# A 31-tap depthwise convolution split into even and odd phases: three half-length chains on VectorE

## What is computed

```
xn = RMSNorm(x)
[q|k|v|o|i|f|u|g] = xn @ w_in
branch A: mLSTM, 4 heads x 256, chunks of tokens in turn (w = exp(logd - m_tok), C_new = decay*C + ...)
branch B: glu = u[..., :1024] * sigmoid(u[..., 1024:])
          c, conv_buf = causal_dwconv(glu, conv_buf, conv_dw, conv_b)     # width 31, per channel
          c = silu(layernorm(c)); yb = c @ w_proj_b + b_proj_b
merge, output projection, residual, then an FFN: up-projection, depthwise conv of width 3, gelu gate, down
```

## Time and profile before

| | |
|---|---|
| time, median of 3 runs | 1942.17 us (1935.84, 1942.17, 1943.59) |
| span of the profiled execution | 1933.8 us, 31692 instructions |
| TensorE | busy 1914.8 us, 99% |
| VectorE | busy 1308.3 us, 68%; 331.7 us of it in L2241 |
| ScalarE | busy 817.0 us, 42% |
| the chain that ended last | TensorE 90%, VectorE 6%, ScalarE 2% |

### The profile page before, as it was taken

How to read it: one execution, slowest core, us unless ns; L and a number is a source line. 1 busy time by engine, 2 the same in 40 slices (tenths; PEclk the granted TensorE clock), 3 DMA queues, 4 the chain that set the end, 5 groups by cost and what they waited for, 6 DMA issues and landing times.

```text
span 1933.8 us, 31692 instructions
## 1 busy us (share of the span) xinstructions
PE 1914.8 (99%) x12999; PEld 1891.8 (98%) x12999; DVE 1308.3 (68%) x1767; ACT 817.0 (42%) x1512; POOL 81.2 (4%) x138
## 2 busy tenths in 40 slices
PE   9999999999999999999999999999999999999997
PEld 8999999999999999999999999999999999999997
DVE  7788779878788745355444458977777777646363
ACT  5454443233232234474122345655445444645342
POOL 0000001111111111110000000000000000000000
PEclk9999999999999999999999999999999999999999
DMA  3323234343333446659231314222122222556554
GB/s 134 129 97 128 75 126 105 89 100 86 96 92 93 109 118 195 197 171 325 104 136 44 128 39 139 73 84 79 68 89 76 71 79 98 202 189 215 203 175 154
DMA packets 100463, 237.57 MB, mean 123 GB/s; under 512 B 16348, under 2 KB 51548, under 8 KB 100320
## 3 DMA queue, kind: packets, MB, share of 16 engines
q1 hardware_dynamic: 89088, 194.65, 29.6%
q0 software_dynamic: 11232, 40.90, 9.3%
HBM read 182.92 MB, written 52.59 MB: 122 GB/s over the span
## 4 chain that ended last, share of the span: by engine, by line
PE 90%; DVE 6%; ACT 2%; issue 1%; DMA 1%; SPq 0%; POOL 0%; DVEq 0%; ACTq 0%; POOLq 0%
PE ps L1013 14%; PE ps L1015 14%; PE ps L1014 14%; PE ps L1370 7%; PE ps L1371 7%; PE ps L1372 7%; PE ps L1388 4%; PE ps L1390 4%; PE ps L1389 4%; PE ps L1170 3%; PE ps L1171 3%; PE ps L1172 3%; PE ps L1102 1%; PE ps L1099 1%; PE ps L1082 1%
## 5 line engine op out<-in xcount | busy, mean ns | idle before, releaser
L1013 PE MATMUL ps<-rx,fhi 128*128 128x364 f32 (+2 forms) x1312 | 438.8, 334 | 1.0 <-DMA flo<-wts 0.6
L1015 PE MATMUL ps<-rx,flo 128*128 128x364 f32 (+2 forms) x1312 | 427.5, 326 | 0.0
L1014 PE MATMUL ps<-rx,fhi 128*128 128x364 f32 (+2 forms) x1312 | 427.5, 326 | 0.0
L2241 DVE SCALAR_TENSOR_TENSOR cacc<-glub,pars,cacc 128x1118 f32<-128x1118 f32 x240 | 331.7, 1382 | 6.7
L1013 PEld LDWEIGHTS ps<-rx,fhi 128*128 128x128 f32 x1312 | 246.8, 188 | 3.3 <-ACT spl L1560 1.6
L1014 PEld LDWEIGHTS ps<-rx,fhi 128*128 128x128 f32 x1312 | 246.9, 188 | 1.5
L1015 PEld LDWEIGHTS ps<-rx,flo 128*128 128x128 f32 x1312 | 246.6, 188 | 0.0
L1388 PE MATMUL ps<-ghi,dhi 128*128 128x384 f32 (+1 forms) x528 | 173.6, 329 | 1.9 <-DVE glo L2669 1.6
L1390 PE MATMUL ps<-ghi,dlo 128*128 128x384 f32 (+1 forms) x528 | 172.6, 327 | 0.0
L1389 PE MATMUL ps<-glo,dhi 128*128 128x384 f32 (+1 forms) x528 | 172.6, 327 | 0.0
L2662 DVE TENSOR_TENSOR dlo<-draw,dhi 128x1408 fp32r<-128x1408 f32 x48 | 77.7, 1624 | 118.2 <-ACT dhi L1944 118.2
(11 more groups left out here) (339 smaller groups left out, 4839.8 us busy)
## 6 DMA issues: line engine op xcount, KB each, us to landing
draw<-wdn SPq DMA_DIRECT2D x48, 704.0 KB, 4.2
uraw<-wts SPq DMA_DIRECT2D x44, 512.0 KB, 4.3
fhi<-wts POOLq DMA_DIRECT2D x39, 512.0 KB, 6.4
flo<-wts POOLq DMA_DIRECT2D x39, 512.0 KB, 5.6
fraw<-wts SPq DMA_DIRECT2D x27, 512.0 KB, 3.6
scr_g<-cva SPq DMA_DIRECT2D x22, 512.0 KB, 2.6
araw<-wts SPq DMA_DIRECT2D x36, 256.0 KB, 2.7
graw<-scr_g SPq DMA_DIRECT2D x43, 192.0 KB, 4.1
```

Of the source, the lines that this page charges most:

```text
L1013: pe.matmul(b, hi[:, w], src[:, his[k], cols], start=(k == 0), stop=False)
L1014: pe.matmul(b, hi[:, w], src[:, los[k], cols], start=False, stop=False)
L1015: mm = pe.matmul(b, lo[:, w], src[:, his[k], cols], start=False, stop=(k == KB - 1))
L2241: op = dve.scalar_tensor_tensor(a[:, :], g[:, j:j + AW], pars[:, at:at + 1], a[:, :], ALU.mult, ALU.add)
```

## The change

The convolution is computed in two phases. With E = g at even positions and O = g at odd positions (574 each, `GH`), and w0 the 16 even-numbered and w1 the 15 odd-numbered taps, three sums of half length (559, `AH`) are kept:

- f_a = sum of w0[i] * E[m + i] (16 taps)
- f_d = sum of w1[i] * O[m + i] (15 taps, 560 long)
- f_e = sum of (w0[i] + w1[i - 1]) * (E + O)[m + i] (16 taps), on the sum f_s = E + O formed once per block

Even results are f_a[m] + f_d[m] + b; odd results are f_e[m] + b - f_d[m + 1] - f_a[m]. The tap sums `hsum` are formed once at the start. A block is now `NOP` = 51 operations of half length where it was 31 of full length. E and O are read by stride 2 (8 bytes) out of `glub`, and the last two operations write `cacc` by stride 2; f_a, f_d, f_e and f_s are contiguous. The three chains take turns, and each operation waits for the one three back, its own chain's last.

Further: there is one `cacc` in place of two, and the last two operations of block k wait for the store of block k - 1; the row `nb` is now two buffers of [128, 128], loaded for each step two steps ahead by a DMA of 64 KB (36 of them in place of 4, each behind a wait for VectorE's `w_neg`); `TAPS_AT` puts 6 operations ahead of the pair stage, 6 into pair 0, 11 into each other pair and 2 behind it; blocks 2 to 7 put 3 or 4 operations into each slot; `conv_fin` counts two per block.

```diff
@@ constants
+CE = (CW + 1) // 2
+CO = CW // 2
+NOP = 1 + CE + CO + CE + 3
+GH = GW // 2
+AH = AW // 2
-TAPS_AT = [4] + [7 + 6 * i for i in range(NB)]
+TAPS_AT = [6] + [12 + 11 * i for i in range(NB)]
...
-            return [(k, i * CW // CONV_SLOTS, (i + 1) * CW // CONV_SLOTS)]
+            return [(k, i * NOP // CONV_SLOTS, (i + 1) * NOP // CONV_SLOTS)]
...
@@ SyncE
             def store_conv(j):
-                sp.wait_ge(conv_fin, j + 1)
+                sp.wait_ge(conv_fin, 2 * j + 2)
...
+            def load_nb(i):
+                h, j = STEPS[i]
+                sp.dma_start(nb[i % 2][:, :], scr_neg[h][step_cols(j)].partition_broadcast(P)).then_inc(nb_in[i % 2], 16)
...
                     h, j = STEPS[i]
-                    if j == NCHUNK and h + 1 < NH:
+                    if i + 2 < len(STEPS):
                         sp.wait_ge(w_neg, i + 1)
-                        sp.dma_start(nb[:, :], scr_neg[h + 1].partition_broadcast(P)).then_inc(nb_in, 16)
+                        load_nb(i + 2)
...
@@ VectorE
             rest(0)
             x_norm(0), x_rest(0)
+            dwt = pars[:, PDW:PFF].rearrange("p (k j) -> p k j", j=CW)
+            dve.tensor_copy(hsum[:, :, 0:1], dwt[:, :, 0:1]).then_inc(half_set, 1)
+            dve.tensor_tensor(hsum[:, :, 1:CE], dwt[:, :, 1:CW - 1:2], dwt[:, :, 2:CW:2], ALU.add).then_inc(half_set, 1)
             rest(1), rest(2)
...
+            def conv_op(k, n):
+                g = glub[k % 2]
+                g0, g1 = g[:, 0:GW:2], g[:, 1:GW:2]
+                even, odd = cacc[:, 0:AW:2], cacc[:, 1:AW:2]
+                done = (NOP - 2) * k
+                at, q = PDW + k * CW, PV["convb"] + k
+                bias = pars[:, q:q + 1]
+                if n == 0:
...
+                    dve.tensor_tensor(f_s[:, :], g0, g1, ALU.add).then_inc(tap, 1)
+                elif n < NOP - 3:
+                    i, chain = divmod(n - 1, 3)
+                    if i == CE - 1 and chain == 1:
+                        chain = 2
+                    acc, src, w, tapw = (
+                        (f_a, g0, AH, pars[:, at + 2 * i:at + 2 * i + 1]),
+                        (f_d, g1, AH + 1, pars[:, at + 2 * i + 1:at + 2 * i + 2]),
+                        (f_e, f_s, AH, hsum[:, k, i:i + 1]))[chain]
+                    if i:
+                        dve.wait_ge(tap, done + (n - 2 if (i, chain) != (CE - 1, 2) else n - 1))
+                        dve.scalar_tensor_tensor(acc[:, :], src[:, i:i + w], tapw, acc[:, :], ALU.mult, ALU.add).then_inc(tap, 1)
...
+                elif n == NOP - 2:
+                    if k:
+                        dve.wait_ge(c_sto[(k - 1) % 2], 32 * ((k + 1) // 2))
+                        dve.wait_ge(csum_set, k)
+                    dve.scalar_tensor_tensor(even, f_a[:, :], bias, f_d[:, 0:AH], ALU.add, ALU.add).then_inc(conv_fin, 1)
+                else:
+                    dve.wait_ge(tap, done + NOP - 2)
+                    dve.tensor_tensor(odd, f_e[:, :], f_a[:, :], ALU.subtract).then_inc(conv_fin, 1)
```

More of the change, by code:

```diff
@@ L188, in taps_of @@
     while t0 < t1:
-        k, j = divmod(t0, CW)
-        n = min(CW - j, t1 - t0)
+        k, j = divmod(t0, NOP)
+        n = min(NOP - j, t1 - t0)
         yield k, j, j + n
@@ L196, in taps_at @@
     if S_B <= s < S_B + 4:
-        at, rest = TAPS_AT[NB], 2 * CW - TAPS_AT[NB]
+        at, rest = TAPS_AT[NB], 2 * NOP - TAPS_AT[NB]
         return list(taps_of(at + rest * (s - S_B) // 4, at + rest * (s - S_B + 1) // 4))
@@ L396, in build @@
     glub = [room(f"glub{s}", [P, GW]) for s in range(2)]
-    cacc0 = room("cacc0", [P, AW])
+    cacc = room("cacc", [P, AW])
+    f_s = room("f_s", [P, GH])
+    hsum = room("hsum", [P, KB, CE])
     assert room.at <= at_w
@@ L413, in build @@
     sm = [room(f"sm{s}", [P, 8]) for s in range(2)]
-    nb = room("nb", [P, T])
+    nb = [room(f"nb{s}", [P, L]) for s in range(2)]
     rst = [Room(room.at + 4 * XW * c)(f"rst{c}", [P, XW]) for c in range(XN)]
-    cacc = [cacc0, room("cacc1", [P, AW])]
+    f_a = room("f_a", [P, AH])
+    f_e = room("f_e", [P, AH])
+    f_d = room("f_d", [P, AH + 1])
     early = (room.at - at_s) // blk
@@ L540, in build @@
         gt_set = sem("gt_set")
-        nb_in = sem("nb_in")
+        nb_in = [sem(f"nb_in{s}") for s in range(2)]
         cb_in = sem("cb_in")
@@ L665, in store_conv @@
             def store_conv(j):
-                sp.wait_ge(conv_fin, j + 1)
+                sp.wait_ge(conv_fin, 2 * j + 2)
                 sp.dma_start(conv_tail[0][:, j, :], glub[j % 2][:, SEQ:SEQ + HALO]).then_inc(tail_out[j % 2], 16)
                 sp.dma_start(conv_tail[1][:, j, :], glub[j % 2][:, GW - HALO:GW]).then_inc(tail_out[j % 2], 16)
-                sp.dma_start(scr_c[j][:, 0:SEQ], cacc[j % 2][:, 0:SEQ]).then_inc(c_sto[j % 2], 16)
-                sp.dma_start(scr_c[j][:, SEQ:T], cacc[j % 2][:, AS0:AW]).then_inc(c_sto[j % 2], 16)
+                sp.dma_start(scr_c[j][:, 0:SEQ], cacc[:, 0:SEQ]).then_inc(c_sto[j % 2], 16)
+                sp.dma_start(scr_c[j][:, SEQ:T], cacc[:, AS0:AW]).then_inc(c_sto[j % 2], 16)
             def pairs():
@@ L732, in _ @@
                 if s == GATE_END + 12:
-                    sp.wait_ge(drow_set, 2)
+                    sp.wait_ge(gate_dve, 16)
                     sp.dma_start(scr_dec, drow[:, :]).then_inc(dec_out, 16)
                     sp.wait_ge(neg_out, 16)
-                    sp.dma_start(nb[:, :], scr_neg[0].partition_broadcast(P)).then_inc(nb_in, 16)
+                    load_nb(0), load_nb(1)
                     sp.dma_start(cb[1][:, :, :], c_in[:, 0]).then_inc(cb_in, 16)
@@ L789, in _ @@
                         sp.wait_ge(c_sto[j], C_STORED)
+                    for j in range(2):
                         sp.dma_start(cs[j][:, :], scr_c[j]).then_inc(cs_in[j], 16)
@@ L2161, in exponents @@
                 at = 16 * j + h
-                dve.scalar_tensor_tensor(wt[p][:, :], nb[:, step_cols(j)], gt[:, at:at + 1], mask[:, :], ALU.add, ALU.min)\
+                dve.scalar_tensor_tensor(wt[p][:, :], nb[p][:, :], gt[:, at:at + 1], mask[:, :], ALU.add, ALU.min)\
                     .then_inc(w_neg, 1)
@@ L2224, in gated @@
                         .then_inc(glu_set, 1)
-            taps_done = [0]
-            def taps(k, j0, j1):
-                g, a = glub[k % 2], cacc[k % 2]
-                for j in range(j0, j1):
-                    at = PDW + k * CW + j
-                    if j == 0:
-                        dve.wait_ge(glu_set, 2 * k + 2)
-                        if k >= 2:
-                            dve.wait_ge(c_sto[k % 2], 32 * (k // 2))
-                            dve.wait_ge(csum_set, k - 1)
-                        q = PV["convb"] + k
-                        op = dve.tensor_scalar(a[:, :], g[:, 0:AW], pars[:, at:at + 1], pars[:, q:q + 1], ALU.mult, ALU.add)
-                    else:
-                        dve.wait_ge(tap, taps_done[0])
-                        op = dve.scalar_tensor_tensor(a[:, :], g[:, j:j + AW], pars[:, at:at + 1], a[:, :],
-                                                      ALU.mult, ALU.add)
-                    if j < CW - 1:
-                        op.then_inc(tap, 1)
-                        taps_done[0] += 1
-                    else:
-                        op.then_inc(conv_fin, 1)
+            def conv_op(k, n):
[6 more added lines that the diff above has]
+                if n == 0:
+                    dve.wait_ge(glu_set, 2 * k + 2)
+                    dve.wait_ge(half_set, 7)
+                    if k:
+                        dve.wait_ge(conv_fin, 2 * k)
+                    dve.tensor_tensor(f_s[:, :], g0, g1, ALU.add).then_inc(tap, 1)
[10 more added lines that the diff above has]
+                        dve.scalar_tensor_tensor(acc[:, :], src[:, i:i + w], tapw, acc[:, :], ALU.mult, ALU.add).then_inc(tap, 1)
+                    else:
+                        if chain == 2:
+                            dve.wait_ge(tap, done + 1)
+                        dve.tensor_scalar(acc[:, :], src[:, i:i + w], tapw, None, ALU.mult).then_inc(tap, 1)
+                elif n == NOP - 3:
+                    dve.wait_ge(tap, done + NOP - 3)
+                    dve.scalar_tensor_tensor(f_e[:, :], f_e[:, :], bias, f_d[:, 1:AH + 1], ALU.add, ALU.subtract).then_inc(tap, 1)
+                elif n == NOP - 2:
+                    if k:
+                        dve.wait_ge(c_sto[(k - 1) % 2], 32 * ((k + 1) // 2))
[4 more added lines that the diff above has]
+                    dve.tensor_tensor(odd, f_e[:, :], f_a[:, :], ALU.subtract).then_inc(conv_fin, 1)
@@ L2249, in add_sum, with taps @@
+            def taps(k, n0, n1):
+                for n in range(n0, n1):
+                    conv_op(k, n)
             def add_sum(k):
-                dve.wait_ge(conv_fin, k + 1)
+                dve.wait_ge(conv_fin, 2 * k + 2)
                 if k:
                     dve.wait_ge(csum_set, k)
```

(4 more changed lines are left out.)

18 lines of the change are left out of this document (8 added, 10 removed).

## The result

The changed kernel takes 1941.88 us (median of 20 runs, 1936.59 to 1945.81); the kernel before, run beside it 20 times, 1937.14 us (1935.83 to 1943.63). The ratio is 1.0017, 95% interval 1.0009 to 1.0025: slower by 0.17%, some 3 us. (This ratio is not that of the two medians, which lie 4.7 us apart, 0.24%; the two means lie 3.7 us apart. A quarter of the runs of the kernel before lie near 1942, and its median doesn't show them.) That is inside the 0.5% that the forecast called "same", and the range of 1933 to 1950 held it, but the interval is clear of 1 and the sum had said -0.1 us. The agreement of 1942.0 with 1941.88 is an accident. The median of three from which the forecast started, 1942.17, lay 5 us above that of a larger set; the change then added about as much to the typical run.

What follows compares the result with a forecast made beforehand. TensorE, busy 1914.8 of 1933.8 us, was taken as the bound. Terms of 0 + 0.1 - 0.2 = -0.1 us left the span at 1933.8; the median, 8.4 us above it, was forecast at 1942 us, range 1933 to 1950.

Steps and rivals of the forecast that it cites:

- the sum: Profiled execution's total: 0 + 0.1 - 0.2 = -0.1 us, bounds -0.4 and +1.4 us without a cost of stride.
- Cost of one operation: Convolution on VectorE: 0.71 us per half-length operation (0.58 for columns, 0.13 fixed), against 1.42 us per full-length tap.
- The near end for the stride: Convolution operands on VectorE: reading every second word costs nothing, 0.71 us; the far end is 1.42 us.
- A: Convolution on VectorE: stride costs some, 1.06 us per strided operation, VectorE still fits; +3 us, 1945 us; chance 0.14.
- B: Convolution on VectorE: stride halves the rate, 1.42 us, VectorE becomes the bound; 1979 us, up to 2000; chance 0.07.
- C: Convolution chains: turns hide nothing, 0.84 us per operation, VectorE gains 14 us; 1943 us; chance 0.73 together with the forecast.
- VectorE's busy time: Whole kernel: eight blocks save 60 us of VectorE's 1308, leaving it busy near 1250 us.
- No effect from 100 to 688 us: Convolution stretch: TensorE's stream is gap-free from 100 to 680 us, so VectorE's saved time becomes VectorE's idle time.
- Pair 0's wait: Start of the pair stage: six operations take 4.3 us against 4.14, adding 0.1 us to TensorE's wait for v.
- `nb` for each step: SyncE's queue: 32 more issues, about 0.4 us each; tightest load, step 29, hidden by 4.5 us: cost 0.
- The rival on the slower side: B, in VectorE's convolution: strided operations at 1.42 us make VectorE the bound; 1979 us; chance 0.07.
- something not listed: Anywhere in the kernel: an unlisted effect costing over 0.5%; chance 0.02.

Runs made afterwards that it cites:

- nb_alone: The kernel before with only nb loaded per step, two steps ahead, convolution old: 1942.8 us against 1936.8, ratio 1.0025 (1.0016 to 1.0034).

## Why the forecast was right and wrong

- **Cost of one operation: right.** 0.71 us from start to start and 797 ns in the records, forecast 0.71 and 780 to 800. The near end for the stride was the right one: 797 against 796 ns. The Trainium skill, "SBUF — State Buffer" (the note on cachelines under "Door 1"), agrees with the trace; the figure of 1.73 ns a column in the Trainium skill, "Vector Engine (DVE) Microarchitecture Reference" (5.2), which that page gives for hops of 4 KiB, does not carry over to a hop of 8 bytes, where a column takes what f_e's takes. That reading every second word costs nothing was called the weakest choice of the forecast; it held. Rivals A, B and C fall.
- **VectorE's busy time: right.** 1260.1 us, forecast near 1250; the fall of 48 us is a fifth under the 60.
- **No effect from 100 to 688 us: right.** TensorE has no idle time there. Pair 0's wait grew from 0.4 to 0.6 us (forecast +0.1), and the 0.2 us for hn at 688 is gone, as forecast.
- **`nb` for each step: wrong, and this is the step that failed.** The forecast asked whether the load arrives in time for VectorE. It does; no wait of VectorE names `nb`. It named `PASS1` as standing behind the loads, but asked only how long their wait for `w_neg` is ("so this wait is short", which was right), and wrote "Hidden by 4.5 us in the worse case: 0". It did not ask what the issues and the traffic do to the stores and reloads of `PASS1`, and what those share the DMA engines with. The rows for it were at hand: the earlier trace rows show the reload of `cs` at 764.84, one of the same series, and the 8.4 us of the earlier trace rows that small transfers in a row can take. Two links lay behind: store, reload, `cs`, `csq`, hn with 2.0 us in hand before TensorE waits, and a reload only 1.2 us ahead of 1 MB of weights. The term was +3 to +6 us, not 0: the changed kernel is 3 us slower by its ratio and 4.7 by its medians, and nb_alone, which has this part of the change alone, 5 and 6.0 us. With it goes the sign of the sum, -0.1 us.
- **The level: right by accident.** The forecast took the spread of the three runs (7.8 us, with the profiled execution 8.4 under their median) as scatter round one value. The kernel has two kinds of runs, near 1937 and near 1942, and the profile showed the lower: of its 125 runs in all four sets 86 lie under 1938.5 and 25 above 1941, with 14 between. The change moved most runs from one to the other: 17 of 20 lie above 1940.9, against 5 of 20 before.
- **The rivals.** None was this one. The rival on the slower side was sought where the change takes most instructions, VectorE, with the price of a stride. The loads, whose forecast was the least worked out, held the effect. The 0.02 for "something not listed" was for over 0.5% and says nothing of a slowdown of 0.17%.

## What to carry to other kernels

When an edit adds small transfers to a queue, don't ask only when they land; list what is issued behind them, and for each large transfer there, how far ahead of the next heavy one it is issued and how much later it may be ready before the bounding engine waits. A transfer that is ahead by 1 us can double its time when it is pushed behind, so such margins act as steps and not as slopes. And where one of three runs lies 6 us under the other two, more runs are needed to see whether there are two kinds, before a median of three is used as the level.
